# Encoder layer with retention, latent attention and 16 experts on one core: two x tiles kept on chip between stages, eight rather than six row tiles normed in the next-to-last expert

## What is computed

```python
proj = x @ w_in                      # retention q, k, v, gate; latents cq, ckv; rotary key
# retention: four heads, a forward and a backward scan in chunks of 128, group norm, gate
# latent attention: eight heads, softmax over all keys of the group
x = layer_norm(alpha * x + concat(ret, mla) @ w_out)
affinity = softmax(x @ w_router)     # (n, 16)
gates, idx = top_k(affinity.T, 2 * n // 16)          # each expert picks its tokens
h = silu(x[idx] @ w_gate) * (x[idx] @ w_up)
moe = zeros.at[idx].add((h @ w_down) * gates)
out = layer_norm(alpha * x + moe)
```

## Time and profile before

| what | us |
|---|---|
| median of three runs | 3472.21 |
| the profiled execution | 3470.6 |
| its span in the trace | 3468.8 |
| first stage, about | 0 to 472 |
| second stage, about | 472 to 790 |
| attention and output stages | 790 to 1945 |
| routing, then experts 0 to 15 | 1945 to 3443 |
| tail | 3443 to 3469 |

### The profile page before, as it was taken

The page is one execution under the profiler, slowest core; times in us unless marked ns, Lnnn a source line. Parts: engine busy times, 40 slices in busy tenths (PEclk is TensorE's granted clock), DMA queues, the critical chain, the costliest instruction groups (busy, mean ns, idle before and its releaser), DMA issues. The chain is left out here.

```text
span 3468.8 us, 52282 instructions
## 1 busy us (share of the span) xinstructions
PE 3330.2 (96%) x19180; PEld 2875.2 (83%) x19180; DVE 2281.6 (66%) x3951; ACT 1630.0 (47%) x2114; POOL 954.8 (28%) x534
## 2 busy tenths in 40 slices
PE   8999989997999999999899599999999999999997
PEld 7888878885777777777788489999999999999996
DVE  5444457766888888887788855555555555555578
ACT  2111134444777777787444323333333333333477
POOL 2000000004888888888122100011111111111112
PEclk9999999998999999999999799999999999999998
DMA  5223447767223332220344245555555555555676
GB/s 180 99 104 115 142 169 244 262 242 209 40 66 72 68 66 54 41 45 15 126 163 151 104 143 170 176 175 175 168 163 171 175 167 164 172 175 175 210 257 224
DMA packets 350293, 506.17 MB, mean 146 GB/s; under 512 B 108384, under 2 KB 244448, under 8 KB 344912
## 3 DMA queue, kind: packets, MB, share of 16 engines
q1 hardware_dynamic: 336784, 457.39, 40.8%
q0 software_dynamic: 13088, 47.06, 5.8%
q10 hardware_dynamic: 288, 0.00, 0.0%
HBM read 366.03 MB, written 138.36 MB: 145 GB/s over the span
## 5 line engine op out<-in xcount | busy, mean ns | idle before, releaser
L64 PE MATMUL psum<-xeT_hi,w_hi 128*128 128x320 f32 x2048 | 634.7, 310 | 0.0
L66 PE MATMUL psum<-xeT_hi,w_lo 128*128 128x320 f32 x2048 | 633.1, 309 | 0.0
L65 PE MATMUL psum<-xeT_lo,w_hi 128*128 128x320 f32 x2048 | 633.0, 309 | 0.0
L2717 DVE TENSOR_TENSOR w_lo<-shared,w_hi 128x2048 fp32r<-128x2048 f32 x190 | 427.6, 2284 | 32.3 <-ACT w_hi L2552 32.2
L2552 ACT ACTIVATE w_hi<-shared 128x2048 fp32r<-128x2048 f32 x192 | 358.2, 1907 | 186.9 <-PE psum L66 186.9
L64 PEld LDWEIGHTS psum<-xeT_hi,w_hi 128*128 128x128 f32 x2048 | 384.4, 188 | 0.9
L65 PEld LDWEIGHTS psum<-xeT_lo,w_hi 128*128 128x128 f32 x2048 | 384.5, 188 | 0.6
L66 PEld LDWEIGHTS psum<-xeT_hi,w_lo 128*128 128x128 f32 x2048 | 384.5, 188 | 0.0
L2364 POOL DMA_INDIRECT xe<-x,idx_next x48 | 76.8, 1599 | 927.2 <-DVE gate_next L2749 860.7
L1573 DVE TENSOR_REDUCE mx<-psum 128x1 f32<-128x1024 f32 x256 | 311.3, 1219 | 23.9 <-PE psum L1372 20.6
L2781 DVE TENSOR_TENSOR h<-gated,psum 128x320 f32<-128x320 f32 x128 | 62.2, 486 | 330.9 <-PE psum L66 296.6
(11 more groups left out here) (445 smaller groups left out, 7848.6 us busy)
## 6 DMA issues: line engine op xcount, KB each, us to landing
shared<-in_w_gate SPq DMA_DIRECT2D x64, 1024.0 KB, 5.1
shared<-in_w_up SPq DMA_DIRECT2D x64, 1024.0 KB, 9.4
shared<-in_w_down SPq DMA_DIRECT2D x64, 1024.0 KB, 5.1
xT<-xaT SPq DMA_DIRECT2D x20, 1024.0 KB, 6.4
rec<-rec SPq DMA_DIRECT2D x20, 768.0 KB, 3.6
shared<-rec SPq DMA_DIRECT2D x20, 768.0 KB, 5.2
shared<-in_x SPq DMA_DIRECT2D x20, 512.0 KB, 5.4
cq_hi<-xT SPq DMA_DIRECT2D x20, 512.0 KB, 6.2
```

Source lines behind the costliest of these rows:

```text
L64: pe.matmul(out, a[0], b[0], start=first, stop=False)
L65: pe.matmul(out, a[0], b[1], start=False, stop=False)
L66: return pe.matmul(out, a[1], b[0], start=False, stop=last)
L2717: v.tensor_tensor(w_lo[n % 4][:], raw[n % 4], w_hi[n % 4][:].bitcast(F32), ALU.subtract).then_inc(s["lo_made"], 1)
```

## The change

The two buffers of turned x tiles are allocated at the other end of the memory, behind a gap of 56 floats, and live on into the second stage. There u = 0 and u = 1 read them in place, they are neither stored nor loaded, and `uq_hi` and `uq_lo` use their space afterwards. `load_x(0)`, which now loads the rotary table alone, stands behind the three weight loads. In the last stage eight row tiles are normed in expert 14; tiles 0 and 1 lie in `xe`, 2 to 4 in `y`; each `take_y` of the first half waits for the store of its own buffer, the last gather waits for the stores of tiles 0 and 1, and SyncE's order, the slots and the places of the norms are changed. In the diff the two projections `project_gate` and `project_lat`, which now take their operands from `x_parts(u)`, are left out.

```diff
@@ -182,7 +182,10 @@
         x = [c.shared[:, (6 + b) * D:(7 + b) * D] for b in range(2)]
-        xT = [sb(f"xaT{b}", [P, 2, DK, P], F32R) for b in range(2)]
+        c.kept = ExitStack()
+        c.kept.enter_context(nc.sbuf_tensor("gap_right", [P, 56], F32, side="right"))
+        xT = c.last_xT = [c.kept.enter_context(nc.sbuf_tensor(f"xaT{b}", [P, 2, DK, P], F32R, side="right"))
+                          for b in range(2)]
         x_hi, x_lo = ([t[:, a, :, :] for t in xT] for a in range(2))
@@ -261,7 +264,7 @@
                                      ).then_inc(rt_in[1 - b], 16)
-                    if now:
+                    if now and not (isinstance(t, int) and t >= NT - 2):
                         sp.wait_ge(s["x_lo_made"], t + 1)
@@ -274,7 +277,7 @@
                 for b in range(2):
-                    sp.wait_ge(xT_out[b], 16 * (NT // 2))
+                    sp.wait_ge(xT_out[b], 16 * (NT // 2 - 1))
                 sp.wait_ge(early_in, 16 * len(early_weights(c)))
@@ -584,7 +587,8 @@
         w_hi, w_lo = big[:].rearrange("p (k n) -> p k n", k=DK), sb("wb_lo", [P, DK, W], F32R)
-        uq_hi, uq_lo = sb("uq_hi", [P, 2, D], F32R), sb("uq_lo", [P, 2, D], F32R)
+        ph.enter_context(c.kept)
+        uq_hi, uq_lo = (t[:].rearrange("p a k n -> p a (k n)") for t in c.last_xT)
         raw_more = [shared(W)[:, 0:W] for b in range(2)] + [sb("wb_stage2", [P, W + 32])[:, 0:W]]
@@ -605,6 +609,12 @@
         x_lo = [cq_lo[:, 1, b * D:(b + 1) * D].rearrange("p (k n) -> p k n", k=DK) for b in range(2)]
+
+        def x_parts(u):
+
+            if u < 2:
+                return [c.last_xT[(NT - 1 - u) % 2][:, a, :, :] for a in range(2)]
+            return x_hi[u % 2], x_lo[u % 2]
         cq_ring = [[[t[:, 0, k * D + b * 512:k * D + (b + 1) * 512] for t in (cq_hi, cq_lo)] for b in range(2)]
@@ -711,9 +721,10 @@
                 def load_x(u):
-                    for a, dst in ((0, x_hi[u % 2]), (1, x_lo[u % 2])):
-                        sp.dma_start(dst.rearrange("p k n -> p (k n)").bitcast(F32), d["xT"][tile(u)][:, a, :]
-                                     ).then_inc(x_in[u % 2], 16)
+                    if u >= 2:
+                        for a, dst in ((0, x_hi[u % 2]), (1, x_lo[u % 2])):
+                            sp.dma_start(dst.rearrange("p k n -> p (k n)").bitcast(F32), d["xT"][tile(u)][:, a, :]
+                                         ).then_inc(x_in[u % 2], 16)
                     sp.dma_start(rt[u % 4][:].rearrange("p a n -> p (a n)"), rope_rows[tile(u)]
@@ -760,9 +771,9 @@
-                load_x(0)
                 for k in range(len(early), DK):
                     load_raw(k)
+                load_x(0)
                 sp.wait_ge(s["w_lo_made"], 1)
...
@@ -868,10 +879,10 @@
                 def project_first():
-                    pe.wait_ge(x_in[0], 32)
+                    xh, xl = x_parts(0)
                     for k in range(DK):
                         pe.wait_ge(s["w_lo_made"], k + 1)
-                        x_k, first, last = (x_hi[0][:, k, :], x_lo[0][:, k, :]), k == 0, k == DK - 1
+                        x_k, first, last = (xh[:, k, :], xl[:, k, :]), k == 0, k == DK - 1
                         gate_ins = mm3(pe, ps[:, 2, :], x_k, (w_hi[:, k, 0:RW], w_lo[:, k, 0:RW]), first, last)
@@ -891,7 +902,7 @@
                         ins.then_inc(s["crossed"], 1)
-                        pe.wait_ge(x_in[b], 32 * (u // 2 + 1))
+                        wait_from_one(pe, x_in[b], 32 * (u // 2))
                         wait_from_one(pe, s["gated"], u)
@@ -2206,13 +2217,14 @@
         hot_a, hot_b = (hot_p[:].rearrange("p t n -> p (t n)").bitcast(F32)[:, D * b:D * (b + 1)] for b in range(2))
-        buffers = [y[:, b, :] for b in range(3)] + [spare, hot_a, hot_b] + [xe[:, b, :] for b in range(3)] + halves[0:5]
-        HOME = [0, 1, 2, 3, 4, 5, 3, 4, 5, 6, 7, 8, 0, 1, 2, 9, 10, 11, 12, 13, 3, 4, 5]
+        buffers = [y[:, b, :] for b in range(3)] + [spare, hot_a, hot_b] + [xe[:, b, :] for b in range(3)] + halves[0:3]
+        HOME = [6, 7, 0, 1, 2, 3, 4, 5, 3, 4, 5, 6, 7, 8, 0, 1, 2, 9, 10, 11, 3, 4, 5]
         xg = halves[5:8]
...
         NB_ROWS, NALL = NT + 3, NT + 6
-        NEARLY, NLOADED, NSTEPS = 6, 9, 14
-        ADD_SLOT = {(0, 0): 15, (0, 1): 17, (0, 2): 18, (1, 0): 20, (1, 1): 21, (1, 2): 22}
+        NEARLY, NSTEPS = 8, 16
+        NSLOTS = NEARLY - 2
+        ADD_SLOT = {(0, 0): 17, (0, 1): 18, (0, 2): 19, (1, 0): 20, (1, 1): 21, (1, 2): 23}
         PART_SLOT = [ADD_SLOT[0, 2] - 1, ADD_SLOT[1, 2] - 1]
@@ -2309,48 +2321,54 @@
                 sp.wait_ge(s["scattered"], (E - 2) * 48)
+                sp.wait_ge(s["turned"], last * DK)
                 for i in range(4):
                     load_rows(i)
-                for n in range(8, 12):
+                for n in range(8, 10):
+                    load_chunk(E - 2, n)
+                for i in (4, 5):
+                    load_rows(i)
+                for n in range(10, 12):
                     load_chunk(E - 2, n)
...
                     load_chunk(E - 2, n)
+                store_rows(2)
                 sp.wait_ge(s["lists_made"], E)
-                for i in (4, 5):
+                for i in (6, 7):
                     load_rows(i)
-                for i in (2, 3):
-                    store_rows(i)
-                load_rows(6)
+                store_rows(3)
                 for n in range(14, 16):
...
                     store_rows(i)
-                for i in (7, 8):
-                    load_rows(i)
-
-                for n in range(4, 8):
+
+                for n in range(4, 6):
                     load_chunk(last, n)
                 sp.wait_ge(s["scattered"], last * 48)
+                load_rows(8)
+                for i in (6, 7):
+                    store_rows(i)
+                for n in range(6, 8):
+                    load_chunk(last, n)
                 sp.wait_ge(s["turned"], E * DK)
-                for i in (9, 10, 11):
+                for i in (9, 10, 11, 12, 13):
                     load_rows(i)
...
                     load_chunk(last, n)
-                for i in (12, 13, 14):
+                for i in (14, 15, 16):
                     load_rows(i)
-                store_rows(6)
+                for i in (8, 9):
+                    store_rows(i)
                 for n in range(10, 12):
                     load_chunk(last, n)
-                for i in (7, 8):
-                    store_rows(i)
-                for chunk, first, n_rows in ((8, 15, 2), (9, 17, 2), (10, 19, 1)):
+                store_rows(10)
+                for chunk, first, n_rows in ((8, 17, 2), (9, 19, 1)):
                     sp.wait_ge(s["lo_made"], last * CHUNKS + chunk + 1)
...
                         load_rows(i)
-                    store_rows(9 + chunk - 8)
-                for i in range(12, NT):
+                for i in range(11, NT):
                     store_rows(i)
@@ -2360,6 +2378,9 @@
                         wait_apart(g, s["turned"], e * DK, s["g_passed"])
+                    if isinstance(e, int) and e == last:
+                        for i in range(2):
+                            g.wait_ge(stored[HOME[i]], 16)
                     for st, n in ST:
@@ -2402,8 +2423,8 @@
                     if rows_early(e):
-                        for i in range(NLOADED):
-                            if HOME[i] not in HOME[i + 1:NLOADED]:
+                        for i in range(NEARLY):
+                            if HOME[i] not in HOME[i + 1:NEARLY]:
                                 g.wait_ge(x_in[HOME[i]], 16 * visits(i))
@@ -2581,9 +2602,8 @@
                         a.wait_ge(s["kept"], e + 1)
-                        if rows_early(e):
-                            for b in range(3):
-                                a.wait_ge(stored[b], 16)
+                    if half == 0 and rows_early(e):
+                        a.wait_ge(stored[st], 16)
                     cols = slice(512 * half, 512 * (half + 1))
@@ -2629,7 +2649,7 @@
                 def norm_slot(i):
-                    if i + 1 < NALL and i != 3:
+                    if i + 1 < NALL and i + 1 != NSLOTS:
                         add_up(i + 1)
@@ -2673,8 +2693,11 @@
                             a.activation(gated[ff][:], ps[:, ff, 0:SL], ACT.Silu).then_inc(s["silued"], 1)
-                            if rows_early(e) and 2 <= f < 6:
+                            if rows_early(e) and f >= 2:
                                 norm_slot(f - 2)
+                        if rows_early(e) and step == 3:
+                            take_root(4)
+                            take_root(5)
                         ahead(e, step, more)
@@ -2683,8 +2706,8 @@
                         for one in (add_up, square, take_root):
-                            one(4)
-                            one(5)
+                            one(6)
+                            one(7)
                     for st, n in ST:
@@ -2870,13 +2893,13 @@
```

(17 more changed lines are left out.)

## The result

The changed kernel takes **3488.39 us** (median of five runs, 3484.68 to 3490.41) beside 3472.21: slower, the medians lying 16.2 us apart. The ratio formed from all runs is 1.0043, with a 95% interval of 1.0032 to 1.0054. The forecast was 3483.1, slower for the reasons given, 5.3 us too low. The profiled execution has just the median, 3488.39, where the one of before had 3470.6: +17.8.

What follows compares the result with a forecast made beforehand. The prediction took TensorE to set the end up to about 3415 us and VectorE's row norms after it. Terms -4.8 - 3.6 + 5.2 + 1.7 + 9.8 + 2.6 = +10.9 gave 3481.5 profiled, 3483.1 median; range 3464 to 3491.

Steps and rivals of the forecast that it cites:

- Term 1: Opening of the second stage: TensorE starts earlier with x tiles kept on chip, -4.8 us, bounds -3 and -6.7.
- I leave the slow 3.8 us where they are: Second-stage opening: TensorE's half-clock stretch after its first pause stays unchanged; without it 1.9 us more would be gained.
- Term 2: VectorE's norm tail: two fewer row tiles, -5.3, less 1.7 for the last piece's later slot; -3.6 us.
- Term 3: Expert 14: row 4's store, queued behind two chunk loads, delays a y buffer and stalls TensorE, +5.2 us.
- the second stall of 1.0 at piece 3: Expert 14: TensorE stalls once more, 1.0 us, since chunk 0 and its low half stand between pieces.
- Term 4: Expert 14: half-speed clock for 3.4 us after TensorE's pause, +1.7 us, bounds 0 and 1.9.
- Term 5: Expert 15: later additions, scatter and row 9's load delay TensorE's f = 3, +9.8 us, bounds +4.8 and +13.5.
- came through 6.8 us behind the addition: Expert 14's scatter: as before, SyncE's wait for it ends 6.8 us after the second addition, now at 3370.3.
- Term 6: Expert 15: f = 4 can start 9.65 us behind f = 3, which takes 7.05; +2.6 us.
- Rival (a): Only expert 15's stall comes, row 4's store landing within 5.0 us: +4.0, 3476.2 us; chance 0.2.
- Rival (b): Rows arrive in time, row 9 by 3374.4, so only the opening and tail gains remain: -8.4, 3463.8; chance 0.2.
- Rival (c): Opening's gain is eaten by late weights or first record, TensorE stopping in the first projection: +15.7, 3487.9; chance 0.05.

Runs made afterwards that it cites:

- before again: The kernel before, unchanged, measured and profiled a second time: 3475.58 us.
- e3: Changed kernel with SyncE's store of row 4 ahead of its loads of weight chunks 14 and 15: 3479.08 us.
- e7: As e6, with the last added piece in slot 22 instead of 23: 3463.22 us.
- e10: The changed kernel, unchanged, measured and profiled a second time: 3488.14 us.
- e2: Changed kernel's experts part behind stages 1 and 2 of the kernel before: 3489.27 us.
- e4: Changed kernel with both additions of expert 14's last half ahead of the norms of tiles 6 and 7 on VectorE: 3478.50 us.
- e5: Changed kernel with the edits of both e3 and e4: 3471.89 us.
- e6: As e3, with rows 8 to 11 loaded into free tiles ahead of expert 14's scatter: 3467.42 us.
- e11: Experts part of e7 behind stages 1 and 2 of the kernel before: 3469.16 us.
- e1: Changed kernel's stages 1 and 2 with the experts part of the kernel before: 3468.03 us.

## Why the prediction held, and where it was short

Terms 2 to 6 were to give +15.7 between gather and end; it is +17.0 in the first pair of traces and +16.6 in the second. The terms as measured below add up to +16.4 for the first pair; 0.6 us is not assigned.

- **Term 1**, -4.8: right in place and size for the wait itself. From the first stage's end to the first product it is 2.23 us in all nine traces with the new opening, and 6.3 to 7.2 in the five with the old one. Five pairs of medians that differ only by the opening give 4.8, 3.2, 0.9, 2.3 and 5.9 us, 3.4 in the mean; the 0.9 and the 5.9 compare kernels of different sittings. The step that failed is "I leave the slow 3.8 us where they are": it was 5.8 here, and the slow stretch after it, 3.4 before, was 6.8. Half of these 5.4 us is 2.7, and 2.0 were lost: 361.8 us from the first product to attention's first addition on POOL, where the kernel before took 359.75. But before again has 362.05 and e3 357.5, each with the slow time given above, so this is a wander of the clock that the step took for fixed. That the new opening lengthens it was not shown (means: 360.8 in nine traces, 359.9 in five).
- **Term 2**, -3.6: -2.9, which is -5.28 + 1.6 + 0.79. Both parts taken were right: two norms are 5.28, and 139.4 - 5.3 = 134.1 is what e7 reaches (134.2). The slot cost 1.6 (forecast 1.7). Missing was a wait for the gathered rows: the second addition of expert 15 now stands four norms behind the last low chunk, which releases POOL's gather, and not five (it is in slot 18, right behind the first in slot 17; they were in 15 and 17). The load that used to be covered is late by up to 1.5, 0.79 in the changed kernel.
- **Term 3**, +5.2: 4.00. Right queue, right buffer, right landing (9.1 us for a forecast 9.3), the second stall of 1.0 at piece 3 did not come. The size varies: 3.43 us in e10, 4.51 in e2. **Term 4**, +1.7: 1.5. By the rule cited from the Trainium skill ("TensorE: Matmul & The Clock Gate", Part 1) each new pause costs a slow stretch; the trace agrees, at both pauses. It does not hold for every pause: in e3 the one of 2.93 us ahead of 493.26 had none behind it (1.00 from 481.6 to 505.0), and the changed kernel's clock was at 0.50 around the same pause.
- **Term 5**, +9.8: 11.5. The step that failed is the scatter that "came through 6.8 us behind the addition": it was 8.8. The third part took 4.94 where it had 1.45, 3.5 more, and from its end to SyncE's next load of rows it took 3.0 us where it had taken 4.5, 1.5 less. This second part is 3.0 to 3.3 in the changed kernel, e10, e3, e4 and e5, and 4.1 to 5.8 in the four traces with the experts of before, where SyncE had issued chunks 6 and 7 in the same microseconds; that these loads lengthen it was not tested. The landing of row 9 was 8.3 for a forecast 8.4. **Term 6**, +2.6: 0.39 of waiting and 1.9 of slow clock, 2.3. Its own parts, 2.6 and 7.27, make 9.9 and not 9.65, so the forecast had 0.2 too little here.
- Rival (a) needed row 4 to land in 5 us; it took 9.1. Rival (b) needed row 9 by 3374.4; ScalarE had it at 3392.77. e6 shows that order decides here: both stalls go with the same transfers. Rival (c), the opening eaten, names 3487.9, the number nearest to the result, but that is chance: ScalarE took the sixth slice at 478.87 without waiting, and TensorE ran without a gap from 476.60 until the pause ahead of 493.36.

The profiled execution is 6.9 us above its forecast (+17.8 for +10.9). 1.3 of them are the terms 2 to 6; most of the rest lies ahead of the experts: 1.85 at the end of the first stage, 2.0 in the projection, and 2.5 in attention and the output stage. This last stretch, from attention's first addition to POOL's first gather for expert 0, took either 1163.8 to 1165.1 or 1167.2 to 1167.8 us in each trace, with either opening and the same instructions (1165.07 in the first trace of before, 1167.58 and 1167.66 in both of the changed kernel). The granted clock tells the two groups apart: near 1650 it was at 0.50 for 20.5 or 23.9 us in the long ones and for 10.2 or 17.1 in the short ones. Why it fell sooner in some executions was not found. So most of the 6.9 us is the clock's wander in this execution, for which the forecast had no term.

## What to carry to other kernels

When row tiles are pulled ahead into a busy stretch, follow what each buffer waits for through the in-order queue: a 512 KB store behind two weight loads held ScalarE for 9 us, and two norms ahead of an addition held a scatter, a queue and in the end TensorE. Issue what frees a buffer, and what others wait for, first; here two such swaps were worth 13.3 us by the ruler, and the variant that loads rows before the scatter was another 5.9 shorter. Judge effects of a few us between marks inside the trace beside the medians of the whole, and look at the granted clock of the stretches in which two traces differ.

## What was not expected of the hardware

POOL's indirect scatter does not run to its end beside VectorE's subtraction with two inputs in SBUF (`w_lo`, 128x2048). Without it a scatter into `acc` takes 1.4 to 1.6 us. Twelve scatters in all the traces began inside that subtraction, and each ended 1.3 to 1.5 us behind the last of the subtractions that stood together, whatever it had waited: in the changed kernel twice (3.67 and 4.94 us long, VectorE done at 3357.77 and 3374.17), and likewise in e3 (4.94), e6 (4.70), e7 (5.31) and e11 (5.02). A start 0.33 us ahead of the instruction escaped it.

Other neighbours narrow down the cause. A norm's instruction of 1.27 us, which also has two inputs in SBUF, held the scatters' third parts of e4 and e5: 1.79 us long, ending 1.33 behind it. An addition with two inputs in SBUF (`y<-y,shared`, 64x512) did the same in e1 and before again (2.01 and 2.04 us long, ending 1.47 behind it, where the same part takes 1.59). Beside `xeT_lo`, with one input in PSUM, 202 scatters took 1.57 to 1.59, as without a neighbour. So two inputs in SBUF fit every row; no run took one input away from the same instruction.

The Trainium skill, "SBUF — State Buffer", section "SBUF: two separate sides", says that VectorE and GpSimd share a port pair as an exclusive lock, which VectorE takes in a two-port performance mode or, against a GpSimd instruction that reads SBUF, with two inputs in SBUF. For POOL's transfers it names the performance mode alone as what keeps their descriptors from being written. The rows agree with the lock and with the two inputs (the scatter takes its row numbers from the tile `idx`); that the performance mode is what counts they do not show.

TensorE's clock can fall inside the small products at the end of the first stage without any change there: from 465.5 to 469.0 it was 0.55 in the changed kernel's trace, 1.00 in the first of before, and 0.50 in before again.
